# Products of constants in TensorE's waits: ends of the expert phases, mixer starts, behind the ranks

## The reference

```python
for layer in range(DEPTH):                       # first model: m = 0, 1
    h = modulate(rms_norm(x, norm_mix[layer]), sh_m, sc_m)
    mix = even_mixer(h, ...) if layer % 2 == 0 else gla_mixer(h, ...)
    x = x + gt_m[:, None, :] * mix
    h = modulate(rms_norm(x, norm_ffn[layer]), sh_f, sc_f)
    x = x + gt_f[:, None, :] * hier_moe(h, ...)
x = rms_norm(x, final_norm)
for l in range(DEPTH):                           # second model: m = 2, 3
    mix = _token_mixer(x, ...)
    x = _layernorm(alpha * x + mix, ln1_g[l], ln1_b[l])
    ffn = _hier_moe(x, ...)
    x = _layernorm(alpha * x + ffn, ln2_g[l], ln2_b[l])
```

## Time and profile before

| | us |
|---|---|
| median of 3 runs (2389.97 to 2392.21) | 2391.49 |
| the profiled execution | 2389.14 |
| its span, first to last instruction | 2387.5 |
| PE busy in the span | 2092.9 |
| mean granted TensorE clock | 0.988 of full |

### The profile page before, as it was taken

The page is one execution under the profiler, slowest core; times in us unless marked ns, Lnnn a source line. Parts: engine busy times, 40 slices in busy tenths (PEclk is TensorE's granted clock), DMA queues, the critical chain, the costliest instruction groups (busy, mean ns, idle before and its releaser), DMA issues.

```text
span 2387.5 us, 31163 instructions
## 1 busy us (share of the span) xinstructions
PE 2092.9 (88%) x13416; PEld 1321.9 (55%) x13417; DVE 666.0 (28%) x1420; ACT 426.4 (18%) x830; POOL 0.2 (0%) x4
## 2 busy tenths in 40 slices
PE   6998998676767999967667799999998999999996
PEld 4785744332334684423233378886554678885553
DVE  4884331010102223101001244313211543224222
ACT  3142121000001312101000024212111234103111
POOL 0000000000000000000000000000000000000000
PEclk9999999999999999999999999999999999999999
DMA  9756789999999447999999942219999542249996
GB/s 401 294 227 271 311 331 425 426 426 426 426 426 426 170 179 304 425 426 426 427 426 426 426 171 99 106 71 396 416 424 425 246 176 106 106 190 405 424 424 267
DMA packets 68663, 770.16 MB, mean 323 GB/s; under 512 B 7616, under 2 KB 8128, under 8 KB 10176
## 3 DMA queue, kind: packets, MB, share of 16 engines
q1 hardware_dynamic: 68256, 768.20, 78.0%
q10 hardware_dynamic: 288, 0.26, 0.0%
HBM read 767.38 MB, written 1.05 MB: 322 GB/s over the span
## 4 chain that ended last, share of the span: by engine, by line
PE 68%; DMA 27%; DVE 3%; ACT 1%; issue 1%; SPq 0%; ACTq 0%; DVEq 0%
DMA slab<-in_triples 26%; PE psum L519 17%; PE psum L551 14%; PE psum L2210 8%; PE psum L2242 6%; PE psum L870 5%; PE psum L2124 4%; PE psum L2138 1%; DMA slab<-in_dense 1%; PE psum L622 1%; PE psum L1429 1%; PE psum L2171 1%; PE psum L2150 1%; PE psum L923 1%; PE psum L2184 0%
## 5 line engine op out<-in xcount | busy, mean ns | idle before, releaser
L2210 PE MATMUL psum<-slab 128*32 128x512 f32 (+1 forms) x3840 | 459.8, 600 | 216.6 <-DMA slab<-in_triples 206.3
L519 PE MATMUL psum<-slab 128*128 128x128 f32 (+4 forms) x2616 | 470.7, 338 | 5.4 <-DVE slab L2025 3.5
L519 PEld LDWEIGHTS psum<-slab 128*128 128x128 f32 (+1 forms) x2616 | 385.2, 191 | 108.7 <-issue 73.3
L2210 PEld LDWEIGHTS psum<-slab 128*32 128x32 f32 x3840 | 148.6, 110 | 523.4 <-DMA slab<-in_triples 310.4
L551 PE MATMUL psum<-slab 128*128 128x256 f32 x1504 | 334.2, 382 | 5.2 <-ACT slab L2431 2.3
L551 PEld LDWEIGHTS psum<-slab 128*128 128x128 f32 x1504 | 286.4, 191 | 51.5 <-issue 9.7
L2242 PE MATMUL psum<-slab 128*32 128x512 f32 (+1 forms) x1920 | 223.2, 596 | 2.0 <-DMA slab<-in_triples 2.0
L2281 DVE TENSOR_TENSOR slab<-psum,slab 128x512 f32<-128x512 f32 (+1 forms) x44 | 24.6, 558 | 636.6 <-PE psum L2210 485.6
L2124 PE MATMUL psum<-slab 128*128 128x256 f32 x704 | 167.9, 380 | 1.2 <-DVE slab L2285 1.2
L2124 PEld LDWEIGHTS psum<-slab 128*128 128x128 f32 x704 | 126.1, 189 | 20.9 <-issue 5.0
L2251 ACT ACTIVATE slab<-psum,slab 128x128 f32<-128x128 f32 x176 | 66.1, 456 | 317.7 <-PE psum L519 317.7
(11 more groups left out here) (445 smaller groups left out, 1420.4 us busy)
## 6 DMA issues: line engine op xcount, KB each, us to landing
slab<-in_triples SPq DMA_DIRECT2D x360, 1536.0 KB, 26.3
slab<-in_dense SPq DMA_DIRECT2D x73, 2048.0 KB, 10.3
slab<-in_pairs SPq DMA_DIRECT2D x14, 2048.0 KB, 9.1
slab<-in_pairs SPq DMA_DIRECT2D x4, 1024.0 KB, 26.7
slab<-in_dense SPq DMA_DIRECT2D x2, 1680.0 KB, 29.8
slab<-in_vec SPq DMA_DIRECT2D x1, 2589.5 KB, 33.0
slab<-in_pairs SPq DMA_DIRECT2D x8, 256.0 KB, 26.0
slab<-in_pairs SPq DMA_DIRECT2D x4, 512.0 KB, 9.9
```

What stands on the lines that cost most here:

```text
L519: ins = mm(out_ap, lhs, rhs, start=(n == 0), stop=(n == len(pairs) - 1), skip_group_check=True)
L2210: ins = mm(psum[WIN * g:WIN * g + WIN, n, :], xg[:, k, WIN * g:WIN * g + WIN], weights_of(w, j, g, extra), start=(k == 0), stop=(k == KD - ...
```

## The change

Products of constants are added at four kinds of place. Nothing is taken away, and no wait is added or moved.

- Start: four products of the identity with the first two blocks of `xT`, between the modulation vectors and `pe_even`, into bank 7.
- Ranks: two products by `pe_warm` behind `pe_ranks`, ahead of `pe_gather`, for each m.
- Finish, first: five products by `pe_warm` behind the last `pe_sum_turn`, ahead of the wait for `scale_ready`, for each m.
- Finish, second: behind the spreading of the scales, ahead of the next mixer's first product: 2, 1 and 5 products for m = 0, 1 and 2, none for m = 3.

```diff
@@ pe_finish
             pe_sum_turn(q, 2)
             pe_sum_turn(q, 3)
+            pe_warm(7, 5)
             q.e.wait_ge(sems["scale_ready"], q.due("scale_ready"))
             for n, col in enumerate((invs,) if m < 2 else (invs, nmean)):
                 for t in range(NT):
                     ins = mm(psum[:, 4, S * n + P * t:S * n + P * t + P], col[:, t:t + 1].broadcast_to([P, P]), ident,
                              start=True, stop=True)
             ins.then_inc(sems["rows_ready"], 1)
+            if m < 3:
+                pe_warm(7, (2, 1, 5)[m])
@@ pe_moe
             pe_ranks(q, rbank)
+            pe_warm((1, 1, 3)[min(m, 2)], 2)
             pe_gather(q, gated.rearrange("p t a b -> p t (a b)"))
@@ the tensor program, l == 0
                     pe_ada_end(q)
+                    for _ in range(4):
+                        mm(psum[:, 7, :], ident, xT[:, 0:2, :].rearrange("p k n -> p (k n)"), start=True, stop=True, skip_group_check=True)
                     pe_even(q)
```

## The result

| | before | changed |
|---|---|---|
| median of 11 runs each, us | 2391.13 | 2399.90 |
| lowest to highest | 2387.09 to 2395.66 | 2393.37 to 2404.21 |
| ratio (95% interval) | | 1.0033 (1.0024 to 1.0042) |
| profiled execution (span) | 2389.14 (2387.5) | 2400.44 (2398.8) |

The change makes the kernel 0.33% slower, 7.9 us (5.7 to 10.0 by the interval). On the 2391.49 of the prediction the ratio gives 2399.4; the bare median of 2399.9 stands 0.1 above the upper end of the range. The forecast was 2396.0.

The account below looks back on a forecast made before the run. Chain of waits 68% TensorE, 27% DMA; weights pace mid-expert phases, TensorE the mixers. Start +1.3, ranks -0.4, ends +1.8, -0.1, +0.9, +1.0 sum to +4.5 us: 2393.6 profiled, 2396.0 median; range 2392.5 to 2399.8.

Parts of the forecast that it names:

- start: Ahead of the first mixer: four products make the first real product 1.55 us late, 0.25 regained; cost +1.3 us.
- ranks, lateness: Behind the ranks: two products in 1.0 us free make the gather 0.7 us late, four times, +2.8 us.
- ranks, clock regained in the gathers: Gathers of m = 0 and 1: added products keep full clock, -1.62 us each; nothing for m = 2 and 3.
- ends of m = 0, 1, 2, 3: Ends of expert phases: late scales and second fill, less clock and queue gains; +0.9, -0.1, +1.0, +1.8 us.
- the third rival: Ranks: the half-clock stretch may be missing elsewhere or fall anyway, so no 3.2 us back; +7.7 us, 2399.2; chance 0.25.
- Price and place of the products: All added products: 0.43 us per instruction, 0.86 per product at full clock, set against the length of each wait.
- the other rule: Skill's formula for one 512-column instruction: N/2.4 + 2.5 ns, 216 ns; five products would take 2.2 us and fit.
- the rival in which the products fit: All places: at 0.21 us per instruction nothing is late and the clock returns 8.5 us; 2383.0; chance 0.05.
- the rival in which the clock gives back more: Five half-clock stretches, 23.3 us: half, 11.7, returned against 13.2 lateness; +1.5 us, 2393.0; chance 0.10.
- the clock at this point is already back, so nothing is won: Start, ahead of the first mixer: no clock gain was booked against the +1.3 us cost.
- -1.62 for m = 0 and for m = 1: Gathers behind the ranks: 5.46 us mostly at half clock in m = 0, 3.84 at full clock; 1.62 regained each.
- the second rival: Waits further down absorb the ranks' 2.8 and the start's 1.3 us; +0.4 us, 2391.9; chance 0.15.

Follow-up runs that it names:

- before_again: The unchanged kernel before, profiled a second time: 2391.87 us, one execution.
- start_only: Only the four products at the start added to the kernel before: 2391.15 us, ratio 1.0001.
- finish_only: Only the products at the ends of the expert phases (five, then 2, 1 and 5) added to the kernel before: 2395.60 us, ratio 1.0016.
- ranks_only: Only the two products behind the ranks added to the kernel before, in each pass: 2394.07 us, ratio 1.0012.
- ranks_again: Second measurement of the kernel before with only the two products behind the ranks: 2396.07 us against 2391.12, ratio 1.0017.
- before_pad23: The kernel before with 23 tiny products (92 instructions) at the head of TensorE's program: 2398.05 us against 2393.50, ratio 1.0021.
- after_pad41: The changed kernel with 41 tiny products (164 instructions) at the head of TensorE's program: 2406.06 us, ratio 1.0058 to the kernel before.
- after_again: The changed kernel, unaltered, profiled a second time: 2396.59 us, one execution.

## Why the prediction was near, and what it lacked

| term | predicted, us | shown by the traces, us |
|---|---|---|
| start | +1.3 | +0.5 against the first trace; +0.5 to -1.5 against all |
| ranks, lateness | +2.8 | +2.8 (0.76, 0.76, 0.66, 0.66) |
| ranks, clock regained in the gathers | -3.2 | -3.4 against the first trace, -1.8 on average |
| ends of m = 0, 1, 2, 3 | +0.9, -0.1, +1.0, +1.8 | +0.95, +0.1, +1.2, +1.9 |
| stall in the last triples of m = 2 and 3 | none | +2.3, +0.4 |
| sum | +4.5 | +8.4, with +0.5 and -1.8 (measured +7.9, 5.7 to 10.0) |

The result lies 3.4 us above the forecast and within 0.2 us of the 2399.2 of the third rival. That is luck: the rival gets there by 3.2 us that the clock doesn't give back, the runs by half of that and by a stall that no sentence of the prediction foresaw. The first mixer's own spread can be left out of the check: from the ranks of m = 0 to the last instruction the two traces of the changed kernel take 2082.0 and 2083.0 us, those of `before`, `before_again` and `start_only` 2076.1, 2071.8 and 2075.7. That is 8.0 more on the mean, where the terms behind the start sum to 7.9.

**Price and place of the products: right.** One instruction takes 0.43 us; ten take 4.46 with the tail. By the other rule (Trainium skill, TensorE: Matmul & The Clock Gate, section Back-to-back issue gap) ten would take 2.2 us; the row decides, and the rival in which the products fit is out. That it turns on the fit is shown from the other side: cut to the wait, the same kind of products makes the kernel 0.2% faster.

**The ends: right in each of four places**, within 0.2 us, and again in `finish_only`. This doesn't hang on the first trace. From the last turn to the 81st matmul instruction of the next mixer, the six traces of kernels without added products there take 22.2 to 23.4, 23.3 to 24.7 and 25.9 to 26.7 us (m = 0, 1, 2), the four with them 23.9, 23.5 and 27.3 in each. What came back there is 0.9, 1.8 and 2.4 us for m = 0, 1 and 2 (gross lateness 1.85, 1.86 and 3.59 less net), where 0.9, 1.9 and 2.5 were booked. So the rival in which the clock gives back more is out as well.

**Start: over-sized, and its clock was misjudged.** The products began at 32.16 us, not at 33.27, since the part ahead of them ends at another time in each execution (in `ranks_only`, which has none of these products, the first L551 is 1.09 us earlier than in the trace of before). And "the clock at this point is already back, so nothing is won" holds for the first trace alone. In the six other traces without start products or pads, the granted clock is 0.50 in a stretch that begins at 34.8 to 36.4 us, and the 32 instructions take 8.61 to 8.86 us and end at 42.9 to 44.3. With the four products ahead they take 7.10 or 7.11 and end at 42.8 (42.3 in the first trace of before). So the term is anything from +0.5 to -1.5, by the trace that it is set against; `start_only` can't be told from no change (-1.9 to +2.2).

**Ranks: the step that failed in part is "-1.62 for m = 0 and for m = 1".** It took the half clock in both gathers as part of the kernel before. In the seven traces of kernels without products behind the ranks, the gather of m = 0 is at half clock in two and that of m = 1 in five: 7 of 14. In the six with such products it is at full clock in all 12. So the products do hold the clock, as I took it, but they regain 1.73 us in half of the cases and 0.11 in the other half, on average 1.8 for the two gathers. The ranks' sum is then +1.0, in place of -0.4. That is about half of the third rival (clock gives back less), whose doubt was that the stretch "may be missing in other executions". The two timed runs of this part alone, +2.9 and +4.1 us, lie above that, the second also beyond its interval (1.7 at the low end). From the ranks of m = 0 to the end, the traces of `ranks_only` and `ranks_again` take 2075.7 and 2075.2 us, 1.0 more than the mean of the three above, so what the timed runs have more isn't in these traces behind the ranks. It stays open; the half-clock stretches of the first mixer may be some of it, since each costs 1.4 to 3.3 us and the profiled execution of `ranks_again`, one of the quick ones, has none at 52 to 58 us. With one trace for nine runs that is only argued.

**The stall: lacking from the sum.** No term allowed for instructions that cost time by their number. `before_pad23` shows that the count alone brings it, `after_pad41` that it goes when the count is moved on, and the kernels of the table that it stands at one place of the code. That TensorE waits there for its code is argued and not shown. Its 2.7 us are most of the 3.4 by which the result lies above the forecast's +4.5; beside it the ranks are 1.4 higher, the ends 0.5 higher and the start 0.8 lower than booked.

**The lateness isn't absorbed** (the second rival): what the ranks of m = 0 and 1 leave stays through the DMA-bound phase within 1 us, as the earlier trace rows made likely, and the 5.05 us wait of the earlier trace rows takes up nothing, as VectorE is as late as TensorE.

**The two profiled executions differ by more than the kernels.** Their spans are 11.3 us apart, 3.4 more than the ratio. The first trace of before had no half clock in the first mixer at 51 us (clock 1.00 in the row below), the changed kernel's has; likewise at 232 us, 1.00 before and 0.50 changed. They cost 3.3 and 1.4 us, nearly all of the 4.9 us that `after_again` hasn't got:

```profile
51.50:58.10 6.60, 6.60 (x36) 5.85 (x36) 5.00 (x11) 5.68 (x8) 0.00 (x0) 1.00 1.00 422
```

## What to carry to other kernels

A product that keeps the clock up must end before what it covers: measure its duration in the trace of the same shape and type, count it against each wait, and leave some tenths free; here the version with 2 in a wait of 2.5 us gains 0.2%, the one with 5 (and products at other places) loses 0.3%. Before a half-clock stretch is booked as a gain, look for it in a second execution: at the ends of the expert phases it was in both traces of the kernel before, at the gathers in one. And when code is added or taken away ahead of a branch, look at TensorE's "issue" idle time behind it, far from the edit. Look for it in the kernel before as well: here it stood there twice, 10.3 us, more than this change, or any part or size of it without pads, moved the time.

## What the runs showed of the hardware that was not expected

- At the last triple of m = 2, TensorE stood still for 1.2 to 4.7 us at a fixed place of its instruction stream behind a branch, with no wait open that the profile shows. In the four traces with 2.4 us or more the granted clock was 0.50 afterwards (row 1850.30:1853.50). With 0 to 24 instructions added ahead (weight loads counted) it didn't show, with 36 to 92 it grew from 1.23 to 4.68 us, with 256 it was gone. At m = 0 and 1 the kernel before has it with 5.06 and 5.25 us.
- Tiny products at the head of the program are dear: 23 of them (92 instructions) put the first real product off by 9.9 us, 41 (164 instructions) by 15.9 us (21.56 and 27.51 against 11.66 in the first trace of before).
- Half-clock stretches of the same code come and go between executions (at 51 to 60 us, 232 to 238 us, and at the gathers), each worth 1.4 to 3.3 us. Two or three of them make the whole effect that was to be measured, and that is why one pair of traces doesn't size it.
